# Two prompt units turned ahead of the decode outputs, gate tiles at other units, and parameters inside the first projection

## What is computed

```
xn = rmsnorm(h, g_attn);  z = xn @ w_in          # queries, keys, values, S5 input u, merge gates ga, gb
a  = nsa(q, k, v)                                # compressed, selected and window attention, gated, 8 heads
y  = ssm_scan(u)                                 # diagonal complex state space, 32 groups
b  = (gelu(y) @ w_glu1) * sigmoid(gelu(y) @ w_glu2)
h += (sigmoid(ga) * (a @ w_a) + sigmoid(gb) * b) @ w_o
h += (gelu(conv(gate)) * value) @ w_down         # gate, value = rmsnorm(h, g_ffn) @ w_up
h += sigmoid(rmsnorm(h, g_ple) @ w_ple_gate) * (p @ w_ple)
```

## Time and profile before

| | us |
|---|---|
| median of 3 runs | 1131.73 (1131.67 to 1132.99) |
| the profiled execution | 1136.89 |
| its span, first to last instruction | 1135.0 |
| TensorE busy | 1101.8 |
| VectorE busy | 476.3 |
| ScalarE busy | 288.9 |
| GpSimd busy | 167.9 |

### The profile page before, as it was taken

How to read it: one execution, slowest core, us unless ns; L and a number is a source line. 1 busy time by engine, 2 the same in 40 slices (tenths; PEclk the granted TensorE clock), 3 DMA queues, 4 the chain that set the end, 5 groups by cost and what they waited for, 6 DMA issues and landing times.

```text
span 1135.0 us, 16873 instructions
## 1 busy us (share of the span) xinstructions
PE 1101.8 (97%) x6495; PEld 910.0 (80%) x6495; DVE 476.3 (42%) x1201; ACT 288.9 (25%) x931; POOL 167.9 (15%) x290
## 2 busy tenths in 40 slices
PE   7999999999999999999999999999999999999996
PEld 5888776688888888888888778767888888888885
DVE  5999616523422222242435863472334222210032
ACT  4446334401211111110344462352112111100021
POOL 4763601003000000106003623000000000010000
PEclk9999998999999999999999999999999999999998
DMA  9654853146555553444555368323355555444441
GB/s 245 188 146 105 251 166 92 61 147 161 148 148 149 148 148 102 134 138 150 185 158 149 112 173 275 69 93 101 125 148 146 149 148 148 126 128 143 130 145 39
DMA packets 240833, 162.27 MB, mean 143 GB/s; under 512 B 25708, under 2 KB 234848, under 8 KB 240674
## 3 DMA queue, kind: packets, MB, share of 16 engines
q1 hardware_dynamic: 230946, 145.50, 44.6%
q0 software_dynamic: 5056, 13.50, 4.0%
q10 hardware_dynamic: 4752, 2.20, 0.8%
HBM read 157.94 MB, written 7.58 MB: 146 GB/s over the span
## 4 chain that ended last, share of the span: by engine, by line
PE 86%; DVE 8%; ACT 2%; issue 2%; DMA 1%; SPq 1%; DVEq 0%; ACTq 0%
PE bank_act L705 40%; PE bank_dve L705 37%; DVE kT L1827 1%; PE bank_dve L1021 1%; PE bank_act L1096 1%; PE bank_o L1111 1%; DVE pcw L1834 1%; DVE Sf L1816 1%; PE bank_o L1063 1%; DVE vpast L1830 1%; DVE vpast L1824 1%; DVE Sf L1831 1%; DMA R<-in_x_prompt_dram 1%; PE bank_act L895 1%; PE bank_o L1107 0%
## 5 line engine op out<-in xcount | busy, mean ns | idle before, releaser
L705 PE MATMUL bank_act<-xn,ring 128*128 128x264 f32 x1568 | 368.8, 392 | 2.7 <-DVE xn L1791 1.8
L705 PEld LDWEIGHTS bank_act<-xn,ring 128*128 128x128 f32 x1568 | 300.1, 193 | 60.3 <-issue 6.3
L705 PE MATMUL bank_dve<-R,ring 128*128 128x264 f32 x704 | 157.6, 386 | 0.0
L705 PE MATMUL bank_dve<-xn,ring 128*128 128x264 f32 x672 | 156.4, 386 | 0.0
L705 PEld LDWEIGHTS bank_dve<-R,ring 128*128 128x128 f32 x704 | 133.4, 190 | 22.5
L705 PEld LDWEIGHTS bank_dve<-xn,ring 128*128 128x128 f32 x672 | 127.7, 190 | 21.8
L2011 DVE TENSOR_SCALAR PT<-GX,PT 128x264 f32<-128x264 f32 x44 | 18.4, 417 | 200.5 <-ACT GX L1254 200.4
L1254 ACT ACTIVATE GX<-bank_act 128x264 f32<-128x264 f32 x44 | 17.2, 391 | 269.0 <-PE bank_act L705 269.0
L654 POOL DMA_DIRECT2D out_dram<-kall x2 | 1.1, 548 | 445.4 <-ACT kall L1254 445.4
L1254 ACT ACTIVATE xn<-hT 128x264 f32<-128x264 f32 x32 | 13.6, 423 | 202.7 <-DVE hT L2030 150.5
L1254 ACT ACTIVATE PT<-bank_act 128x10 f32<-128x10 f32 (+4 forms) x94 | 29.5, 314 | 127.8 <-PE bank_act L705 123.8
(11 more groups left out here) (373 smaller groups left out, 1358.9 us busy)
## 6 DMA issues: line engine op xcount, KB each, us to landing
ring<-in_w_up_dram SPq DMA_DIRECT2D x88, 512.0 KB, 5.1
ring<-in_w_in_dram SPq DMA_DIRECT2D x28, 1024.0 KB, 6.0
ring<-in_w_down_dram SPq DMA_DIRECT2D x32, 704.0 KB, 4.6
ring<-in_w_glu_dram SPq DMA_DIRECT2D x16, 512.0 KB, 4.4
ring<-in_w_o_dram SPq DMA_DIRECT2D x8, 1024.0 KB, 5.1
ring<-in_w_ple_gate_dram SPq DMA_DIRECT2D x8, 1024.0 KB, 5.2
PT<-in_cache_cmp_dram SPq DMA_DIRECT2D x64, 64.0 KB, 2.6
ring<-in_w_a_dram SPq DMA_DIRECT2D x8, 512.0 KB, 7.0
```

What stands on the lines that cost most here:

```text
L705: ins = pe.matmul(out, lhsT, rhs, start=(k == 0), stop=(k == nk - 1))
```

## The change

Four edits. The parameters of layer 0 are turned inside job 0, after four of its eight k-steps, and count as the layer's own first VectorE job. Scores of unit 2 stand ahead of the first gate tile of the head stage; units 0 and 1 are turned ahead of the decode outputs, with the scores of units 4 and 5 between them. Gate tiles stand ahead of units 4, 8 and 12 and ahead of the last head output. For the third norm the `warm` activation stands ahead of the eight copies.

```diff
 OUTPUTS_AT = ((6, 7, 8, 9, 10, 12, 13, 14), (5, 6, 7, 8, 9, 10, 11, 12))
 DOWN_PREP = (0, 3, 5)
 PAGES_AT = ({8: (2,), 9: (3,), 11: (4, 5), 12: (6, 7)}, {8: (2, 3), 9: (4,), 11: (5, 6), 12: (7,)})
-GATES_IN_HEADS = (1, 5, 9, 13)
+GATES_IN_HEADS = (4, 8, 12, 16)
+U_FIRST = 2
 ROOT_AT = (15, 15)
 SQUARES_AT = ((13, 13), (12, 13))
 
 
-ACT_PRO, DVE_PRO = 4, 6
+ACT_PRO, DVE_PRO = 4, 5
 BANKS, ACT_BANKS = 3, 4
 
 
...
     return offsets((
         ("qkv", 3 * len(QW_CHUNKS) + 2 * NB + 4 + 4 * own + 2 * len(GATES_AT[L])), ("pe", 1), ("states", 1),
         ("gates_rotary", 2), ("turn_qk", 8), ("cmp", 1), ("gate_cmp", 1), ("hidden", 2),
-        ("v_cmp", 3), ("gate_softmax", 1), ("s_probs", 2), ("gate_out", 1), ("p_cmp", 1), ("s_out", 1), ("p_probs", 2 * H + len(GATES_IN_HEADS)), ("glu", KD), ("conv", 1),
+        ("v_cmp", 3), ("gate_softmax", 1), ("s_probs", 2), ("gate_out", 1), ("p_first", U_FIRST), ("p_cmp", 1), ("s_out", 1), ("p_probs", 2 * H - U_FIRST + len(GATES_IN_HEADS)), ("glu", KD), ("conv", 1),
         ("ple_in", 2), ("up", KF), ("gate_rows", 1), ("next_b", 4 * coming), ("ple", KD), ("ple_gate", KD)))
 
 
 def dve_stages(L):
     own, coming = L == 0, L + 1 < DEPTH
     return offsets((
-        ("norm0", 1), ("c", 2 * own), ("k0", own), ("h0", own),
+        ("params", own), ("norm0", 1), ("c", 2 * own), ("k0", own), ("h0", own),
         ("drive", ST), ("s_gates", 1), ("k_cmp", 1), ("s_scores", 2), ("c_scores", 2), ("p_scores", 2 * H), ("w_a", KD), ("glu", KD), ("w_o", KD),
         ("norm1", 1), ("up", KF), ("down", KD + 5 * coming), ("norm2", 1), ("result", 3 * (not coming))))
 
...
 
 
 def params_taken(L):
-    return 6 if L == 0 else dve_jobs(L - 1, "down", DOWN_PREP[0] + 1 + 1)
+    return dve_jobs(0, "params", 1) if L == 0 else dve_jobs(L - 1, "down", DOWN_PREP[0] + 1 + 1)
 
 
 def direct_taken(L):
...
 
 def probs_turned(L, u):
 
-    return act_jobs(L, "p_probs", u + 1 + sum(v <= u for v in GATES_IN_HEADS))
+    if u < U_FIRST:
+        return act_jobs(L, "p_first", u + 1)
+    return act_jobs(L, "p_probs", u - U_FIRST + 1 + sum(v <= u for v in GATES_IN_HEADS))
 
 
 def weight_chunks(L):
...
                     for t in range(2):
                         pe.transpose(bank[:, t * P:t * P + P], xrows[:, t, k * P:k * P + P], ident)
                     pe.transpose(bank[:, SEQ:NT], xrows[0:NB, 2, k * P:k * P + P], ident[0:NB, 0:NB]).then_inc(act_ready if k % 2 == 0 else dve_ready, 1)
-                params_turned(0, dve_bank)
 
             def layer(L, act_bank, dve_bank, next_chunk, mm):
 
...
                         bank = act_bank()
                         rows = hgT if jobs <= U_AT else [xn[:, k, :] for k in range(KD)]
                         for k in range(KD):
+                            if L + jobs == 0 and k == KD // 2:
+                                params_turned(0, dve_bank)
                             if jobs == 0:
                                 pe.wait_ge(hg_ready, 2 * L * KD + k + 1)
                             if t < 2:
...
                                 last.then_inc(dve_ready, 1)
 
                 head_scores(1)
+                head_scores(2)
                 gates(1)
 
 
...
                 for b in range(2):
                     last = pe.transpose(bank[0:NB, P * (b + 1):P * (b + 2)], snew[:, b, :], ident)
                 last.then_inc(act_ready, 1)
-                head_scores(2)
                 head_scores(3)
                 gates(1)
+
+                def turn_probs(u):
+                    t = unit(u)[1]
+                    pe.wait_ge(p_prob, L * 16 + u + 1)
+                    bank = act_bank()
+                    for b in range(2):
+                        for k in range(t + 1):
+                            c = ((t + 1) * b + k) * P
+                            last = pe.transpose(bank[:, c:c + P], S(u)[:, b, P * k:P * k + P], ident)
+                    last.then_inc(act_ready, 1)
+
+                def pair_scores(u):
+                    if u % 2 == 0 and u + 5 < 2 * H:
+                        head_scores(u + 4)
+                        head_scores(u + 5)
+
+                for u in range(U_FIRST):
+                    turn_probs(u)
+                    pair_scores(u)
                 pe.wait_ge(v_in, L * V_LOADS + V_LOADS)
                 pe.wait_ge(act_freed, act_jobs(L, "s_probs", 2))
 
...
                 for half in range(2):
                     last = pe.transpose(bank[:, P * half:P * half + P], o_rows[:, P * half:P * half + P], ident)
                 last.then_inc(act_ready, 1)
-
-                def turn_probs(u):
-                    t = unit(u)[1]
-                    pe.wait_ge(p_prob, L * 16 + u + 1)
-                    bank = act_bank()
-                    for b in range(2):
-                        for k in range(t + 1):
-                            c = ((t + 1) * b + k) * P
-                            last = pe.transpose(bank[:, c:c + P], S(u)[:, b, P * k:P * k + P], ident)
-                    last.then_inc(act_ready, 1)
 
                 def head_out(c):
 
...
                                              start=False, stop=(b == 1), skip_group_check=True)
                     last.then_inc(o_ready, 1)
 
-                for u in range(2 * H):
+                for u in range(U_FIRST, 2 * H):
                     if u in GATES_IN_HEADS:
                         gates(1)
                     turn_probs(u)
-                    if u % 2 == 0 and u + 5 < 2 * H:
-                        head_scores(u + 4)
-                        head_scores(u + 5)
+                    pair_scores(u)
                     if u % 4 == 2 and u >= 6:
                         head_out(u // 4 - 1)
+                gates(1)
                 head_out(H // 2 - 1)
 
 
...
 
             def std(L, i):
 
-                fn(warm[:], c_bias[:, 1:2], ACT.Sqrt)
+                if i < 2:
+                    fn(warm[:], c_bias[:, 1:2], ACT.Sqrt)
 
                 act_.wait_ge(dve_ready, dve_jobs(L, f"norm{i}", 1))
                 bank = bankV[V_AT[L][f"norm{i}"] % BANKS]
...
                 fn(PTs[0:NCMP, 4 * P:5 * P], bank[0:NCMP, 0:P])
                 fn(PTs[0:NB, 5 * P:7 * P], bank[0:NB, P:3 * P]).then_inc(act_freed, 1)
                 exps(1)
+                exps(2)
                 gates(1)
-                exps(2)
+
+                def probs_taken(u):
+                    c, t, g = unit(u)
+                    fn(turned[c % 2][:, g, :, 0:t + 1, P * t:P * t + P],
+                       take(base)[:, 0:2 * P * (t + 1)].rearrange("p (b k q) -> p b k q", b=2, k=t + 1)).then_inc(act_freed, 1)
+
+                for u in range(U_FIRST):
+                    if u > 0:
+                        exps(u + 2)
+                    probs_taken(u)
                 act_.wait_ge(o_ready, L * 5 + 1)
                 fn(o_rows, bankO[:, 0:2 * P]).then_inc(o_taken, 1)
                 fn(pcmp, take(base)[:]).then_inc(act_freed, 1)
...
                               bank[64 * g:64 * g + 64, 0:2 * P].rearrange("p (s x) -> p x s", s=NB)[:, 4 * g:4 * g + 4, :])
                 last.then_inc(act_freed, 1)
 
-                for u in range(2 * H):
-                    if 0 < u < 2 * H - 2:
+                for u in range(U_FIRST, 2 * H):
+                    if u < 2 * H - 2:
                         exps(u + 2)
                     if u in GATES_IN_HEADS:
                         gates(1)
-                    c, t, g = unit(u)
-                    fn(turned[c % 2][:, g, :, 0:t + 1, P * t:P * t + P],
-                       take(base)[:, 0:2 * P * (t + 1)].rearrange("p (b k q) -> p b k q", b=2, k=t + 1)).then_inc(act_freed, 1)
+                    probs_taken(u)
 
                     if u % 4 == 2 and u >= 6:
+                        c = unit(u)[0]
                         act_.wait_ge(o_ready, L * 5 + c + 1)
                         fn(aT[:, c - 1, 0:SEQ], bankO[:, 0:SEQ]).then_inc(o_taken, 1)
+                gates(1)
                 act_.wait_ge(o_ready, L * 5 + 5)
                 fn(aT[:, 3, 0:SEQ], bankO[:, 0:SEQ]).then_inc(o_taken, 1)
 
...
                             angles(L + 1)
                         if o == DOWN_PREP[1]:
                             b_taken(lambda: take(base))
+                fn(warm[:], c_bias[:, 1:2], ACT.Sqrt)
                 for o in range(KD):
                     fn(plT[:, o, :], take(base)[:, 0:NT]).then_inc(act_freed, 1)
                     if o == 1:
...
                 gained(0, 0, k - 1)
                 gained(0, 0, k)
             prep_steps(0)
-            prep_params(0, 0)
+            n[0] = 0
+            prep_params(0, V_BASE[0])
             for k in range(KD):
                 add_squares(0, 0, k)
             prep_angles(0)
             dve.sem_inc(h_done, KD)
             dve.wait_ge(early_in, 16 * EARLY)
             for L in range(DEPTH):
-                n[0] = 0
+                n[0] = V_AT[L]["norm0"]
                 base = V_BASE[L]
                 prm = prm2[:, L]
 
```

## The result

The changed kernel takes 1138.48 us (median of 9 runs, 1134.69 to 1141.79) against 1131.67 us for the kernel before in the same rounds (9 runs, 1127.01 to 1138.06): a ratio of 1.0063 [1.0042, 1.0084]. It is slower, by 0.6%, and lies above the predicted range.

What follows compares the result with a forecast made beforehand. The prediction took the kernel as one stream of matmuls, with TensorE busy for 97% of the span. Heads plus 1.3 and parameters plus 0.5 gave 1.8 us on the median of 1131.73, so 1133.5 us, range 1128.4 to 1136.2.

Steps and rivals of the forecast that it cites:

- heads: waits gone, holes opened: Attention stage, both layers: three waits per layer go, minus 5.3 us; four holes open at turns 6 and 10, plus 6.6.
- scores of unit 2 ahead of the gate tile: Front of the head stage: moved, not added, work; a bank wait of at most 0.15 us, taken as nothing.
- parameters: Kernel start: VectorE copies the parameters later and may delay the sum of squares; plus 0.5 us, from minus 0.1 to 1.4.
- root's table: Third norm: the square-root table is asked for ahead of the copies; TensorE gains nothing, zero.
- clock: Half-clock stretches of 3.41 us, two per layer: old holes go, new ones of the same size come; counted as even.
- my two cases: First projection: started at 12.4, the sum of squares stands where it stood; started at 13.9, it is 1.5 us late.
- The rival with more half clock: Attention stage: new 1.66 us holes bring more half clock; one more stretch gives 1135.2, one per layer 1136.8; chance 0.15.
- its second case: Attention stage: one more half-clock stretch per layer, giving 1136.8 us.
- the prediction's own sign of being wrong: Next profile: the prediction is wrong if, among other signs, half-clock stretches differ in number by two or more.

Runs made afterwards that it cites:

- the parameters back: The changed kernel with the parameters turned ahead of the first projection again, as in the kernel before: 1138.44 us, ratio 1.0057 to the kernel before.
- the parameters alone: The kernel before with the parameters turned inside job 0 and nothing else changed: 1132.20 us, ratio 1.0014 to the kernel before.
- the fill: The changed kernel with three unused matmuls of 256 columns ahead of turns 6 and 10: 1135.37 us, ratio 1.0039 to the kernel before.
- VectorE's order: Weights of unit u made before scores of unit u + 2: 1128.90 us in the changed kernel, 1127.71 us in the kernel before.
- gates at 5, 9, 13 and last: The changed kernel with gate tiles ahead of units 5, 9, 13 and the last output: 1133.65 us, ratio 1.0006 to the kernel before.

## Why the prediction was wrong

The forecast was 1.8 us; the medians of the same rounds differ by 6.8, and the means that are split above by 7.7. By its own terms:

| term | predicted us | measured us |
|---|---|---|
| heads: waits gone, holes opened | +1.3 | +1.1 in the lists of waits, about +0.2 on the path |
| scores of unit 2 ahead of the gate tile | 0 | +1.9 (run), +2.0 (rows) |
| parameters | +0.5 | +0.95 (trace), +1.1 to +1.3 (runs) |
| root's table | 0 | 0 |
| clock | 0 | +3.8 to +4.4 |

**Holes: right.** Both ends came as worked out: no wait at turns 0 to 4 or ahead of the last head output, and four holes of 1.59 us against 1.66. On the path the heads cost less than the lists say: 1.10 us per layer between the traces of the parameters back and the parameters alone, of which about 1.0 is the split of units 2 and 3. That leaves 0.1 where the lists have 0.55. Most of the difference stands unseen in merged rows of the kernel before: the turns of units 7 and 8 behind the head output take 1.00 us (203.27 to 204.27) and those of units 11 and 12 0.91 (212.40 to 213.31), where six such instructions take 0.75 (188.72 to 189.46). The weight load of unit 8 waits there for VectorE, too short for a bracket at the matmul.

**Scores of unit 2: failed.** The sentence "It is moved, not added, work" is wrong. I priced the bank as idle time of TensorE behind unit 1, at most 0.15 us, and neither the partner that unit 2 leaves nor the one that the bank keeps it from. The row for a pair (184.42 us, four instructions in 0.63 us) was there, but a merged row doesn't say that two units ran at once; the starts of single records would have. The Trainium skill (TensorEngine Tiling (Array Packing), Tiling Modes, Key Properties) says that tiles of the array work independently and in parallel. The trace agrees: two units in 1.05 us, one in 1.06.

**Parameters: right mechanism, too small.** The start fell between my two cases, at 13.17, and the sum of squares became late by way of VectorE's additions, as said: between a delay of nothing at 12.4 and of 1.5 us at 13.9 it came out at 0.88. Each of these measures lies in the upper half of the range given, minus 0.1 to plus 1.4; the middle that I took did not follow from a row.

**Clock: failed, and the largest.** "I count the clock as even" compared the number and length of the holes and stopped there. The runs show that a hole of 1.6 us is paid twice: once itself, and, in some executions, by a stretch at half clock behind it. The rival with more half clock was in the text and its mechanism was right, at 0.15, but it was sized by stretches of 3.41 us, one more in all or one more per layer, and the range ended at 1136.2, under the 1136.8 of its second case. Nor does a count of stretches, the prediction's own sign of being wrong, tell what the clock costs: it fell from five (four were counted) to three while the half clock grew. In the changed kernel's trace a stretch lasted 6.82 us, and it did so over scores, head output and turns, up to the gate tile (747.93 to 754.75). The gate tiles at 4, 8 and 12 put exactly this work behind the holes at 6 and 10; before, the stretch behind the hole at 193.18 covered a turn, a pair of scores and then a gate tile. That the holes are the cause of most of it is shown by the fill (path the same, loss 3.4 us smaller) and, less purely, by VectorE's order (no holes, loss 3.3 us smaller). That the kind of work behind a hole sets the length of the stretch is only read from the traces; no run changed that work alone. For it speaks the kernel with gates at 5, 9, 13 and last, where a gate tile starts at 744.92 and the stretch behind the hole lasts 3.41 us (744.00 to 747.41). The third long stretch after the change speaks against it in this plain form: a gate tile runs from 169.67 to 175.70, and the half clock lasts until 174.49.

The Trainium skill's beat that doesn't start with the kernel, which the prediction cites (TensorE: Matmul & The Clock Gate, Part 1, What's actually happening), agrees with the runs. The profile of the parameters alone has the same head stage as before and no half clock in it, that of the parameters back has the holes of after and none behind them, and the runs of the kernel before go from 1126.98 us to 1139.14 in one comparison. So the places aren't fixed; that a beat of the chip's own moves them is not shown. The profiled execution before was one with more stretches than usual, as the prediction supposed, and the median of few runs is a poor measure of an edit of 1 us.

## What to carry to other kernels

Before moving an instruction, look at which instruction starts within some nanoseconds of it: two matmuls over half the rows each can share the array, and one that is moved alone costs its full time. Look at the weight loads too, where a wait can show that the list of the matmuls doesn't have. Where TensorE must wait, price the work behind the wait at half clock too, and rather than covering the wait with a big tile, see whether the engine that is waited for does something less urgent first: one swapped pair of calls in VectorE's loop was worth 4.4 us of path before and 6.9 after. Compare edits by span times granted clock beside the median; over 12 runs it told 1 us apart where the medians didn't.

## What the runs showed of the hardware

- A stretch of half clock can last 6.82 us with TensorE busy throughout (3.41 of 3.41 us in each half): 747.93 to 754.75, 761.59 to 768.41 and 167.67 to 174.49. I had expected work without holes to end it after 3.41.
- Useless matmuls can pay: three of 256 columns in each hole took nothing from the path and won 3.1 us of the median.
- The same hole of 1.59 us was followed by half clock in layer 1 and not in layer 0 of one execution, and nowhere in that of the parameters back.
- Two score matmuls over 64 rows each, on the two halves of the array, take 1.05 us together, and one alone 1.06.
